# A hybrid encoder layer on one core: the first tiles' warm-up, transfers and splits in another order

## What is computed

```python
h = rms_norm(x, norm_mix)
proj = h @ w_in                       # 2048 x 4624
qa, ka, va, qf, kf, vf, f_logit = split(proj)   # widths 1024, 256, 256, 1024, 1024, 1024, 16
out_a = swa_sink_attention(rope(qa), rope(ka), va, sinks)
out_b = forgetting_attention(qf, kf, vf, log_sigmoid(f_logit + b_f))
x = x + concat(out_a, out_b) @ w_o    # 2048 x 2048
h = rms_norm(x, norm_ffn)
u = causal_conv3(h @ w_up) + conv_b   # 2048 x 11264
x = x + (silu(u[:, :5632]) * u[:, 5632:]) @ w_down
out = rms_norm(x, norm_final)
```

## Time and profile before

| | |
|---|---|
| median of 3 runs | 1085.54 us (1084.82 to 1086.59) |
| the profiled execution's own time | 1085.33 us |
| its span, first to last instruction | 1083.5 us |
| granted TensorE clock, mean | 0.996 |
| TensorE matmuls busy | 1073.1 us, 99% |
| TensorE weight loads busy | 925.0 us, 85% |
| VectorE busy | 719.1 us, 66% |
| ScalarE busy | 588.5 us, 54% |
| GpSimd busy | 14.0 us, 1% |
| read from HBM | 199.06 MB, 186 GB/s over the span |

### The profile page before, as it was taken

The page is one execution under the profiler, slowest core; times in us unless marked ns, Lnnn a source line. Parts: engine busy times, 40 slices in busy tenths (PEclk is TensorE's granted clock), DMA queues, the critical chain, the costliest instruction groups (busy, mean ns, idle before and its releaser), DMA issues.

```text
span 1083.5 us, 17806 instructions
## 1 busy us (share of the span) xinstructions
PE 1073.1 (99%) x6131; PEld 925.0 (85%) x6131; DVE 719.1 (66%) x1056; ACT 588.5 (54%) x915; POOL 14.0 (1%) x34
## 2 busy tenths in 40 slices
PE   8999999999999999999999999999999999999997
PEld 8888889898888888888888888888888888888885
DVE  5687666676565777778777777778777444454543
ACT  6956475756455655555556555555555434343432
POOL 1200000000000000000000000000000000000000
PEclk9999999999999999999999999999999999999999
DMA  8776555454555666656665666656666655555562
GB/s 262 205 249 179 172 154 174 135 174 150 180 172 179 188 185 197 186 174 203 189 188 174 199 191 198 186 171 201 192 190 213 212 185 187 193 185 188 190 191 101
DMA packets 169794, 201.66 MB, mean 186 GB/s; under 512 B 8580, under 2 KB 136292, under 8 KB 169632
## 3 DMA queue, kind: packets, MB, share of 16 engines
q1 hardware_dynamic: 168432, 197.48, 58.9%
q0 software_dynamic: 976, 3.37, 0.9%
q10 hardware_dynamic: 352, 0.34, 0.1%
HBM read 199.06 MB, written 2.11 MB: 186 GB/s over the span
## 4 chain that ended last, share of the span: by engine, by line
PE 99%; DMA 0%; DVE 0%; ACT 0%; issue 0%; SPq 0%; DVEq 0%
PE tr_ps L1245 15%; PE pj L1245 15%; PE pj L1004 9%; PE pj L1247 8%; PE tr_ps L1247 8%; PE sc_ps L992 5%; PE sc_ps L994 5%; PE sc_ps L993 5%; PE pj L1006 4%; PE tr_ps L992 4%; PE tr_ps L994 4%; PE tr_ps L993 4%; PE pj L992 3%; PE pj L993 3%; PE pj L994 3%; PE tr_ps L1126 0%
## 5 line engine op out<-in xcount | busy, mean ns | idle before, releaser
L657 DVE TENSOR_TENSOR lo<-raw,hi 128x1024 fp32r<-128x1024 f32 x364 | 440.9, 1223 | 270.1 <-ACT hi L403 269.8
L403 ACT ACTIVATE hi<-raw 128x1024 fp32r<-128x1024 f32 x364 | 380.7, 1058 | 235.3 <-PE sc_ps L994 78.9
L1245 PE MATMUL tr_ps<-act_split,hi 128*128 128x512 f32 x704 | 245.3, 391 | 0.0
L1245 PE MATMUL pj<-act_split,hi 128*128 128x512 f32 x704 | 245.0, 391 | 0.0
L1247 PE MATMUL pj<-act_split,lo 128*128 128x256 f32 x704 | 197.1, 280 | 0.0
L1247 PE MATMUL tr_ps<-act_split,lo 128*128 128x256 f32 x704 | 197.1, 280 | 0.0
L1245 PEld LDWEIGHTS pj<-act_split,hi 128*128 128x128 f32 x704 | 131.6, 187 | 28.9
L1245 PEld LDWEIGHTS tr_ps<-act_split,hi 128*128 128x128 f32 x704 | 131.7, 187 | 28.8
L1004 PE MATMUL pj<-act_split,hi 128*128 128x512 f32 x416 | 147.6, 399 | 0.0
L1247 PEld LDWEIGHTS tr_ps<-act_split,lo 128*128 128x128 f32 x704 | 133.0, 189 | 0.1
L1247 PEld LDWEIGHTS pj<-act_split,lo 128*128 128x128 f32 x704 | 133.1, 189 | 0.0
(11 more groups left out here) (199 smaller groups left out, 1212.3 us busy)
## 6 DMA issues: line engine op xcount, KB each, us to landing
raw<-w_up SPq DMA_DIRECT2D x176, 512.0 KB, 4.2
raw<-w_down SPq DMA_DIRECT2D x88, 512.0 KB, 4.3
raw<-w_in SPq DMA_DIRECT2D x72, 512.0 KB, 3.8
raw<-w_o SPq DMA_DIRECT2D x32, 512.0 KB, 4.1
nat<-x SPq DMA_DIRECT2D x8, 256.0 KB, 5.8
key_bias<-nft_dram POOLq DMA_DIRECT2D x4, 512.0 KB, 8.3
result<-nat SPq DMA_DIRECT2D x7, 256.0 KB, 3.0
gfin<-norm_final POOLq DMA_DIRECT2D x1, 1024.0 KB, 7.9
```

What stands on the lines that cost most here:

```text
L403: act.activation(hi[:, slot, 0:TILE], raw[:, slot, 0:TILE], ACT.Copy).then_inc(hi_done, 1)
L657: dve.tensor_tensor(lo[:, slot, 0:TILE], raw[:, slot, 0:TILE], hi[:, slot, 0:TILE].bitcast(F32), ALU.subtract).then_inc(lo_done, 1)
L1245: pe.matmul(up_banks[v][b].rearrange("p (a n) -> p a n", a=2), wh[:, c, b * P:(b + 1) * P], act_split[:, :, k, :], start=k == 0, stop=Fals ...
```

## The change

TensorE's first warm-up has 10 multiplications instead of 8, the second 5 instead of 6. The gate columns of tile 0 are loaded by ScalarE's queue, behind the identity and ahead of the norm gains, instead of by SyncE's. GpSimd waits for the second quarter of x before it issues its seven small transfers. ScalarE and VectorE take the splits of tiles 1 to 3 in another order: tile 1's four behind piece 7 of x (before: two behind piece 5, two behind piece 7); tile 2's first two ahead of piece 8, its last two behind piece 11; tile 3's likewise around pieces 12 and 15. Tile 0's stay where they are.

```diff
-WARM = 8
-WARM_AGAIN = 6
+WARM = 10
+WARM_AGAIN = 5
+SPLIT_AFTER = {1: (0, 1), 3: (2, 3), 7: (0, 1, 2, 3), 11: (2, 3), 15: (2, 3)}
...
@@ block.sync
                 sp.dma_start(with_gates(raw, c)[:, :, 0:256], win[c][:, :, COL_VA:COL_VA + 256]).then_inc(d_w[c], 16)
-                sp.dma_start(with_gates(raw, c)[:, :, 256:VA_COLS], win[c][:, :, COL_F:COL_F + NH]).then_inc(d_w[c], 16)
+                if c > 0:
+                    sp.dma_start(with_gates(raw, c)[:, :, 256:VA_COLS], win[c][:, :, COL_F:COL_F + NH]).then_inc(d_w[c], 16)
...
@@ block.gpsimd
             pool.memset(ones[:], 1.0).then_inc(ones_s, 1)
+            pool.wait_ge(d_x[1], 32)
             for j in range(3):
...
@@ block.scalar
             act.dma_start(ident[:], ident_c).then_inc(d_id, 16)
+            act.dma_start(with_gates(raw, 0)[:, :, 256:VA_COLS], win[0][:, :, COL_F:COL_F + NH]).then_inc(d_w[0], 16)
             act.dma_start(rows[0:KB, 0], norm_mix.rearrange("a (b p) -> (a b) p", p=P)).then_inc(d_nrm, 16)
...
             for c in range(KB):
+                if c in (8, 12):
+                    split_hi_part(c // 4, 0)
+                    split_hi_part(c // 4, 1)
                 act.wait_ge(x_t, c // 2 + 1)
                 act.activation(act_hi[:, c], x_banks[c][:, 0:S], ACT.Copy,
                                scale=g1[:, c:c + 1]).then_inc(xhi, 1)
-                if c % 2 == 1:
-                    split_hi_part(c // 4, c % 4 - 1)
-                    split_hi_part(c // 4, c % 4)
+                for part in SPLIT_AFTER.get(c, ()):
+                    split_hi_part(c // 4, part)
...
@@ block.vector
             for c in range(KB):
+                if c in (8, 12):
+                    split_lo_part(c // 4, 0)
+                    split_lo_part(c // 4, 1)
                 dve.wait_ge(xhi, c + 1)
...
-                if c % 2 == 1:
-                    split_lo_part(c // 4, c % 4 - 1)
-                    split_lo_part(c // 4, c % 4)
+                for part in SPLIT_AFTER.get(c, ()):
+                    split_lo_part(c // 4, part)
```

## The result

The changed kernel takes 1087.43 us (median of 14 runs, 1085.69 to 1089.14), the kernel before 1085.52 (14 runs, 1084.29 to 1087.42). The ratio is 1.0016, 95% interval 1.0008 to 1.0023: 1.9 us slower, where 0.4 us faster was forecast, and outside the range. The profiled execution took 1087.96 us, span 1086.2.

The account below looks back on a forecast made before the run. Arrival times in the first 26 us were taken to bound the gain: first matmul -0.4, full clock -0.3, order of splits +0.3, together -0.4 us, from 1085.54 to 1085.1, range 1083.8 to 1086.4.

Parts of the forecast that it names:

- the flight of norm_ffn behind the gates: ScalarE's queue at the start: flight stays 5.1 us, issue at 2.2 instead of 1.69, landing at 7.3 instead of 6.8.
- A: Main case at the start: clock holds at 1.00, first matmul at 9.6, sum -0.4 us; chance 0.50.
- rival D: Start: gates hold up norm_ffn, which lands behind 7.6; first matmul 11.6, total 1087.4 us; chance 0.10.
- the bound 7.1: Upper bound in us for norm_ffn's flight, the longest row shown; everything 2.0 later than with 5.1.
- whatever the change does, it does before 26 us.: Whole kernel: behind 26 us TensorE's stream only starts earlier or later, its 1050 us don't change.
- a wait behind 26 us: Sign of being wrong: TensorE was to be busy without a break from 26 us on.
- The clock: TensorE's granted clock, 7.24 to 10.65 us: longer first warm-up may hold it at 1.00 instead of 0.50; full-clock stretch -0.3 us.
- The rule cited against the move: Gates on ScalarE's queue: spreading issues over engines saves only issue time, 0.5 us here; what stands beside them pays.
- The middle value: norm_ffn's flight at the start: 5.1 us, its own row, taken between bounds of 3.9 and 7.1.
- GpSimd held back: Seven small transfers leave the stretch up to 10 us: counted as nothing; last lands by 21.4, needed at 24.28.
- The order: Splits of tiles 1 to 4: +0.7 us at tile 1, -0.26 at tiles 2 and 3, -0.15 at tile 4; +0.3 together.
- First matmul: First projection matmul at the start, 10.02 us before: forecast 9.6 with norm_ffn's flight at 5.1.

Follow-up runs that it names:

- e3: Kernel before with only tile 0's gates moved to ScalarE's queue, ahead of the norm gains: 1089.78 us, ratio 1.0030.
- n_after: Changed kernel without the four key_bias transfers (GpSimd fills zeros): 1086.13 us, against 1084.76 for the kernel before without them.
- n_gates: Kernel before with the gates moved ahead of the gains and no key_bias transfers: 1087.58 us, against 1084.76 for the kernel before without them.
- e10: Kernel before plus a second, unread copy of tile 0's gates on ScalarE's queue, ahead of the norm gains: 1088.88 us, ratio 1.0025.
- e7: Changed kernel with the gates back on SyncE's queue: 1084.83 us, ratio 0.9989 to the kernel before.
- k1: Kernel before with the four key_bias transfers issued one after the other, each when the one before has landed: 1084.98 us, ratio 0.9987.
- e1: Kernel before with the new warm-up counts (10 and 5) alone: 1085.61 us, ratio 0.9991.
- e4: Kernel before with only GpSimd's seven small transfers held back: 1085.80 us, ratio 0.9991.
- e8: Kernel before with the gates on ScalarE's queue and the two norm gains on GpSimd's, ahead of its other transfers: 1087.42 us, ratio 1.0010.
- e9: Kernel before plus a second, unread copy of tile 0's gates on ScalarE's queue, behind the norm gains: 1086.08 us, ratio 1.0002.
- e5: Kernel before with tile 0's gates on ScalarE's queue, behind the norm gains: 1092.78 us, ratio 1.0059.

## Why the prediction was wrong

- **The step that failed: the flight of norm_ffn behind the gates** ("I take 5.1, the same transfer's own row"). The move was priced by its 0.51 us of issue, with the flight unchanged. Behind the gates it flew 5.5 to 6.2 in the profiles of the changed kernel, e3, n_after and n_gates, 6.5 in e10, and landed at 7.7 to 8.8 instead of 7.3. In n_after, n_gates and e10 the clock then stood at 0.50 during most or all of the second warm-up and the first projection matmuls, which A's sum had left out. The mechanism stood in the prediction as rival D, with a chance of 0.10 and the bound 7.1. The landing was behind D's 7.6 in all five. That the median of the changed kernel, 1087.43, is D's 1087.4 is luck in part: the stage and the hold, which D's sum counts as nothing, are in it, and the first matmul came at 10.24 and, in n_after, 11.12, not at D's 11.6. The gates cost 3.3 to 3.7 us alone (e3), 2.8 without the stage (n_gates), 2.6 inside the change (against e7), and their copy 2.8 (e10), where A's sum had the first split only 0.14 us later.
- **The second step that failed: "whatever the change does, it does before 26 us."** It was read from one profile, in which TensorE happened not to wait in the key_bias stage. Eleven of the fourteen kernels in the table have waits there of 0.2 to 2.3 us in their profiles; the other three all have k1's edit. In e1's profile the stage takes back more than the start gained. The prediction named a wait behind 26 us as a sign of being wrong, and it came.
- **The clock: right in the outcome, not in the way.** A's 1.00 between 7.24 and 10.65 came true: with 10 multiplications the second series ran at 0.12 a pass in 7 of 8 profiles, with 8 in 2 of 11. But A had the clock hold over the empty stretch, and in the changed kernel it wasn't up ahead of it: it rose at 6.74 and then stayed. The one profile of the eight in which it fell is n_after, where TensorE stood 1.80 us for norm_ffn. The part alone gained 0.5 us by the medians and 1.0 by the ratio; the sum had 0.7.
- **The rule cited against the move: its hint was right and not followed.** By the Trainium skill, DMA: Bandwidth & Descriptors, section Issuing engines are not separate DMA queues, only the time of the issue is saved. The runs agree in that what stood beside the gates paid: the values of tile 0 landed at 7.9 instead of 7.1, and norm_ffn late. They don't in size: the gates were issued 0.9 us earlier and landed 2.2 us earlier, at 6.1 instead of 8.35. The middle value was then taken from a row in which no small pieces stood ahead of the gains.
- **GpSimd held back: probably too small.** Counted as nothing; alone (e4) it measured 0.3 us by the medians and 1.0 by the ratio, whose interval just touches none. x lands 0.3 earlier there and norm_ffn flies 4.4. The sinks were in time: VectorE never waited for them.
- **The order: right.** Forecast +0.7 at tile 1; from start to start TensorE's gap there is 1.05 instead of 0.26, so 0.8 more. From tile 1 to tile 4 it then takes 10.83 us instead of 11.44, 0.6 less where 0.4 was forecast. Alone it measured 0.9999.
- **First matmul:** 9.6 forecast for A, 10.24 measured; with the gains in time (e1) it is 9.58.

What stays open: how often an execution of the changed kernel loses its time in the stage and how often at the start. One profile shows the first (tile 4 at 25.95, all the loss behind it), and one of the same start the second (n_after, 27.51). e3's profile, 1087.83, lies 2 us under its median and doesn't show all that a usual run pays. Nor is it settled what the remaining 1.0 to 1.4 us of e8 are, or what sets the moment at which the clock rises.

## What to carry to other kernels

A transfer put on a quiet queue is priced by who stands behind it there, not by its issue: here 512 pieces of 64 bytes ahead of an 8 KB transfer that TensorE waits for cost 2.8 us, and behind it nothing, as long as nobody waited for the pieces themselves (e9); where somebody did, 6 us (e5). A bound of an unknown flight deserves a chance when a rule speaks for that side. And a stage with no wait in one profile may be one transfer's luck: compare the flights there before calling the rest of the execution fixed, and where a burst of broadcasts isn't urgent, issue it one at a time. A clock column that says 1.00 is to be checked against the time of a pass.

## What the runs showed of the hardware

The same 32 KB in 512 pieces flew 4.8 to 5.3 us on ScalarE's queue when issued at 1.21, 8.4 to 9.5 when issued at 2.16 behind two transfers of 8 KB, and 6.2 on SyncE's at 2.15: an issue 0.95 us later, with the two transfers ahead, made a landing 4.0 to 5.7 us later. A weight load issued 1.25 us into the burst of four broadcasts flew 11.6 us (the changed kernel), one issued 1.08 us into it 8.7 (before), and none flew over 6.6 when the broadcasts were issued one at a time (k1). And the granted clock fell in the kernel before (0.50 from 7.24), when it had been up since 3.83 and TensorE had stood 1.8 us from 4.40 on; in n_after it fell at 9.19, when TensorE had just stood 1.80 us.
